# Four expert groups' first products in full float, made during the choice of candidates

## The reference

```python
q = (hx @ w_q)...                                  # 8 heads, two half queries each
s = einsum('thpd,pkd->thpk', q, sub_keys)          # scores against 2 x 128 keys
top_s, top_i = lax.top_k(s, 16)                    # 16 best of each half
cand = top_s[..0.., :, None] + top_s[..1.., None, :]
best_s, best_pos = lax.top_k(cand, 16)             # 16 best of the 256 pairs
wts = softmax(best_s)
act = gelu(einsum('td,thkd->thk', hx, u[idx]))     # first product, rows of u
return einsum('thk,thkd->td', wts * act, v[idx])   # second product, rows of v
```

## Time and profile before

| what | us |
|---|---|
| median of 3 runs | 5012.27 (5011.85 to 5012.48) |
| the profiled execution's own time | 5008.28 |
| its span | 5006.4 |
| TensorE busy in the span | 4576.1 (91%) |
| VectorE busy | 2506.5 (50%) |
| ScalarE busy | 1424.7 (28%) |

### The profile page before, as it was taken

One profiled execution on the slowest core, in us unless ns is written; L12 is line 12 of the kernel. 1 busy time (PEld: TensorE's weight loads), 2 busy tenths in 40 slices (PEclk: granted clock), 3 DMA queues, 4 the chain that ended last, 5 costly groups with the idle time before them and its releaser, 6 DMA issues.

```text
span 5006.4 us, 57535 instructions
## 1 busy us (share of the span) xinstructions
PE 4576.1 (91%) x22736; PEld 3778.7 (75%) x22736; DVE 2506.5 (50%) x4265; ACT 1424.7 (28%) x2544; POOL 0.2 (0%) x4
## 2 busy tenths in 40 slices
PE   6999989999985999998999998909799999999997
PEld 5888877888873458667887887809688888888886
DVE  5666572301013324345776111089566666666665
ACT  1000142200002001234443100117455555555553
POOL 0000000000000000000000000000000000000000
PEclk9999999999997999998999999959899999999999
DMA  7888533245323434120000353302554455554552
GB/s 274 306 305 304 214 130 135 101 135 167 135 101 151 151 116 144 68 87 8 1 1 1 139 164 126 128 7 105 210 199 192 187 212 214 202 200 187 197 214 84
DMA packets 135081, 751.61 MB, mean 150 GB/s; under 512 B 12256, under 2 KB 29792, under 8 KB 66144
## 3 DMA queue, kind: packets, MB, share of 16 engines
q1 hardware_dynamic: 134880, 748.79, 40.6%
HBM read 729.86 MB, written 18.87 MB: 150 GB/s over the span
## 4 chain that ended last, share of the span: by engine, by line
PE 63%; DVE 6%; ACT 2%; issue 1%; DMA 1%; DVEq 0%; SPq 0%; ACTq 0%
PE ps L272 15%; PE ps L2665 14%; PE ps L2641 10%; PE ps L2643 5%; PE ps L759 4%; PE ps L2349 2%; PE ps L2580 1%; PE ps L2179 1%; PE ps L2182 1%; PE ps L2572 1%; PE ps L2170 1%; PE ps L299 1%; PE ps L2228 1%; DVE area L309 1%; PE ps L2227 0%
## 5 line engine op out<-in xcount | busy, mean ns | idle before, releaser
L272 PE MATMUL ps<-area,ring 128*128 128x256 f32 (+1 forms) x5280 | 1283.4, 406 | 50.0 <-ACT area L1413 22.1
L272 PEld LDWEIGHTS ps<-area,ring 128*128 128x128 f32 x5280 | 1006.1, 191 | 327.3 <-issue 201.9
L2641 PE MATMUL ps<-hp_parts,pieces 128*128 128x512 f32 x2048 | 728.7, 400 | 33.3 <-DVE pieces L2737 33.3
L2665 PE MATMUL ps<-pieces,gact_parts 128*128 128x512 f32 x3072 | 706.2, 391 | 5.3 <-issue 2.8
L2665 PEld LDWEIGHTS ps<-pieces,gact_parts 128*128 128x128 f32 x3072 | 576.3, 188 | 127.0 <-DVE pieces L2737 3.7
L676 DVE SCALAR_TENSOR_TENSOR area<-ring,area 128x2048 f32<-128x2048 f32 x192 | 432.4, 2289 | 315.0 <-DMA ring<-w_mod_dram 314.7
L2643 PE MATMUL ps<-hp_parts,pieces 128*128 128x256 f32 x2048 | 576.8, 282 | 0.0
L2737 DVE TENSOR_TENSOR pieces<-ring,pieces 128x512 fp32r<-128x512 f32 x512 | 353.4, 691 | 308.9 <-ACT pieces L2682 308.9
L2641 PEld LDWEIGHTS ps<-hp_parts,pieces 128*128 128x128 f32 x2048 | 386.8, 189 | 129.7 <-issue 25.7
L2682 ACT ACTIVATE pieces<-ring 128x512 fp32r<-128x512 f32 x512 | 323.1, 632 | 400.0 <-PE ps L2643 312.8
L2737 DVE TENSOR_TENSOR pieces<-area,pieces 128x512 fp32r<-128x512 f32 x512 | 352.5, 689 | 162.2 <-ACT pieces L2682 153.5
(11 more groups left out here) (410 smaller groups left out, 4218.0 us busy)
## 6 DMA issues: line engine op xcount, KB each, us to landing
ring<-u_dram SPq DMA_DIRECT2D x128, 1024.0 KB, 7.0
area<-v_dram SPq DMA_DIRECT2D x128, 1024.0 KB, 8.5
ring<-w_mod_dram SPq DMA_DIRECT2D x96, 1024.0 KB, 7.0
ring<-w_mg_dram SPq DMA_DIRECT2D x80, 1024.0 KB, 4.8
ring<-w_z_dram SPq DMA_DIRECT2D x77, 1024.0 KB, 4.9
ring<-w_branch_dram SPq DMA_DIRECT2D x80, 512.0 KB, 3.5
ring<-w_out_dram SPq DMA_DIRECT2D x32, 1024.0 KB, 4.8
ring<-w_y_dram SPq DMA_DIRECT2D x20, 1024.0 KB, 4.8
```

The lines of the kernel that those rows point to most:

```text
L272: last = nc.tensor.matmul(bank(slot, 0, n) if out is None else out, ring[:, slot, k * P:(k + 1) * P], rhs(k), start=(k == 0), stop=(k == k ...
L2641: both = nc.tensor.matmul(bank(s).rearrange("p (a t) -> p a t", t=T), piece[:, b, 0, k * P:(k + 1) * P], hp2[:, :, c, :], start=(c == 0), ...
L2665: last = nc.tensor.matmul(out, gact[:, k, ga, s, t * P:(t + 1) * P], piece[:, b, va, :], start=(s == 0 and w == 0), stop=(s == GROUP - 1 a ...
```

## The change

The u phases of groups 0 to 3 (EARLY = 4) are replaced by float32 products with `hp` itself, which TensorE makes right after the scores. Their sums go to banks 0 to 3 and 4 to 7 in turn; ScalarE takes the GELU of each from PSUM into the buffer `x`, between its Exp instructions. x, the residual, is stored to DRAM before and loaded again in group 4. SyncE loads the u rows of groups 1 to 4 as rows are used up. In the expert stage TensorE's order becomes u4, v0, v1, v2, v3, then u5, v4, u6, v5 and so on to u31, v30, v31. `gact_parts` and `hp_parts` change places in memory, so that of hp_parts only 80 columns of the first quarter still lie in the last weight buffer; the split of hp is made in quarters, in the order 1, 2, 3, 0, and only quarter 0 waits for the last store. The clearing of yacc moves behind the remainders of the first u phase.

```diff
+        EARLY = 4
+        early = x[:, :].rearrange("p (g s t) -> p g s t", g=EARLY, t=T)
-        hp_parts, gact_parts, pieces = ...
+        gact_parts, hp_parts, pieces = ...
 # choose_act
+            def early_gelu(g):
+                act.wait_ge(early_made, GROUP * (g + 1))
+                if g == 0:
+                    act.wait_ge(inputs_loaded, (N_INPUTS + 1) * 16)
+                b = GROUP * (g % 2)
+                nc.scalar.activation(early[:, g, :, :], ps[:, b:b + GROUP, 0:T], ACT.Gelu).then_inc(early_kept, 1)
             for r in range(DC // LANES):
+                for g in {0: (0, 1), 2: (2,)}.get(r, ()):
+                    early_gelu(g)
                 ...
+            early_gelu(3)
 # choose_pe, after the scores
+            for g in range(EARLY):
+                for r in range(GROUP):
+                    pe.wait_ge(u_landed[r], g * 16 + 16)
+                    if r == 0 and g < 2:
+                        S["scores"].upto(pe, "act", f"k{4 * g + 3}", 0)
+                    elif r == 0:
+                        pe.wait_ge(early_kept, g - 1)
+                    for c in range(DC):
+                        last = nc.tensor.matmul(bank(GROUP * (g % 2) + r, 0, T), ring[:, r, c * P:(c + 1) * P], hp[:, c, :], start=(c == 0), stop=(c == DC - 1))
+                    last.then_inc(early_made, 1)
+            pe.wait_ge(early_kept, EARLY)
             barrier(pe, "scores", "cand")
 # experts_act
-            for k in range(2):
-                act.wait_ge(w_stored[k], 32)
-            do("rounded", nc.scalar.activation(hp2[:, 0, :, :], hp, ACT.Copy))
-            u_act(act, 0, 0)
-            keep_half(act, 0, PER_PHASE)
-            gelu_act(act, 0)
+            for q in (1, 2, 3, 0):
+                if q == 0:
+                    act.wait_ge(w_stored[1], 32)
+                do(f"r{q}", nc.scalar.activation(hp2[:, 0, 4 * q:4 * q + 4, :], hp[:, 4 * q:4 * q + 4, :], ACT.Copy))
+            u_act(act, EARLY, 0)
             round_gact(act, 0, 0)
+            keep_half(act, EARLY, PER_PHASE)
+            gelu_act(act, EARLY)
 # experts_dve
-            nc.vector.memset(yacc, 0.0).then_inc(zeroed, 1)
             for n in range(PER_PHASE):
                 remainder(dve, n, n, u_source(n))
-            sum_halves(dve, 0)
+            dve.wait_ge(w_stored[0], 32)
+            nc.vector.memset(yacc, 0.0).then_inc(zeroed, 1)
             weigh(dve, 0, 0)
             split_gact(dve, 0, 0)
+            sum_halves(dve, EARLY)
 # the order of phases: a group has a u phase before its v phase only where
+        def has_u(g):
+            return EARLY <= g < NG - 1
 # experts_sp
             load_u(0)
+            barrier(sp, "norm_p")
+            sp.dma_start(a["residual"], x[:, :]).then_inc(inputs_loaded, 16)
+            for g in range(1, EARLY + 1):
+                load_u(g)               # row s waits for early_made >= 4 * (g - 1) + s + 1
             ...
+                if g == EARLY:
+                    sp.wait_ge(gact_split, EARLY)
+                    sp.dma_start(x[:, :], a["residual"]).then_inc(inputs_loaded, 16)
                 if not is_last(g):
                     sp.wait_ge(remainders, v_base(g) + PER_PHASE)
                     load_v(g + 1)
```

More of the change, by code:

```diff
@@ L2616, in is_last, with u_base, after_early, gelu_of @@
             return g >= NG - n
-        def base(g):
-            return g * (2 * PER_PHASE) + PER_PHASE
+        def has_u(g):
+            return EARLY <= g < NG - 1
+        def u_base(g):
+            return PER_PHASE * (1 + EARLY + 2 * (g - EARLY - 1)) if g > EARLY else 0
         def v_base(g):
-            return base(g) + (0 if is_last(g) else PER_PHASE)
+            if g < EARLY:
+                return PER_PHASE * (1 + g)
+            return PER_PHASE * (1 + EARLY + 2 * (g - EARLY) + has_u(g))
+        def after_early(g):
+            return g - EARLY
+        def gelu_of(g):
+            return early[:, g, :, :] if g < EARLY else gel
         def take_piece(pe, p):
@@ L2725, in group @@
                     round_piece(act, v_base(g) + n, n, v_source(n))
-                    if n == 3 and not is_last(g):
+                    if n == 3 and has_u(g):
                         keep_half(act, g + 1, v_base(g))
-                    if n == 6 and not is_last(g):
+                    if n == 6 and has_u(g):
                         gelu_act(act, g + 1)
@@ L2768, in experts_dve @@
             dve.wait_ge(weights_kept, NR)
-            for k in range(2):
-                dve.wait_ge(w_stored[k], 32)
             do = Do(dve, st_hps, "dve")
-            do.wait("act", "rounded")
-            do("rest", nc.vector.tensor_tensor(hp2[:, 1, :, :], hp, hp2[:, 0, :, :].bitcast(F32), ALU.subtract))
+            for q in (1, 2, 3, 0):
+                do.wait("act", f"r{q}")
+                v = slice(4 * q, 4 * q + 4)
+                do(f"l{q}", nc.vector.tensor_tensor(hp2[:, 1, v, :], hp[:, v, :], hp2[:, 0, v, :].bitcast(F32), ALU.subtract))
             do.end()
-            nc.vector.memset(yacc, 0.0).then_inc(zeroed, 1)
             for n in range(PER_PHASE):
                 remainder(dve, n, n, u_source(n))
-            sum_halves(dve, 0)
+            dve.wait_ge(w_stored[0], 32)
+            nc.vector.memset(yacc, 0.0).then_inc(zeroed, 1)
             weigh(dve, 0, 0)
             split_gact(dve, 0, 0)
+            sum_halves(dve, EARLY)
             dve.wait_ge(zeroed, 1)
             def group(g, k):
-                for n in range(0 if is_last(g) else PER_PHASE):
-                    remainder(dve, base(g) + n, n, u_source(n))
-                    if n == LAG and g > 0:
+                for n in range(PER_PHASE if has_u(g) else 0):
+                    remainder(dve, u_base(g + 1) + n, n, u_source(n))
+                    if n == LAG:
                         add(dve, g - 1, 3)
@@ L2789, in group @@
                     remainder(dve, v_base(g) + n, n, v_source(n))
-                    if is_last(g) and n == LAG:
+                    if not has_u(g) and g > 0 and n == LAG:
                         add(dve, g - 1, 3)
@@ L2793, in group @@
                         add(dve, g, n // GROUP - 1)
-                    if n == 4 and not is_last(g):
+                    if n == 4 and has_u(g):
                         sum_halves(dve, g + 1)
@@ L2804, in last_dve @@
         def last_dve(dve):
+            dve.wait_ge(inputs_loaded, (N_INPUTS + 2) * 16)
             do = Do(dve, st_res, "dve")
@@ L2835, in experts_sp, with load_u @@
             sp.dma_start(cut(PC_AT, N_PEER_CONSTS), a["peer_consts"]).then_inc(peer_loaded, 16)
-            def load_u(g, at=None):
+            def load_u(g):
                 for s in range(GROUP):
-                    if at is not None:
-                        sp.wait_ge(remainders, at + (4 * s + 4))
+                    if g > EARLY:
+                        sp.wait_ge(remainders, u_base(g - 1) + (4 * s + 4))
+                    elif g > 0:
+                        sp.wait_ge(early_made, GROUP * (g - 1) + s + 1)
                     sp.dma_start(ring[:, s, 0:D], a["u"][g * GROUP + s]).then_inc(u_landed[s], 16)
```

43 lines of the change are left out of this document (25 added, 18 removed).

## The result

| | before | after |
|---|---|---|
| timed runs, median | 5012.06 (5006.43 to 5012.48) | 4927.82 (4925.16 to 4930.41) |
| the profiled execution's own time | 5008.28 | 4925.83 |
| its span | 5006.4 | 4924.1 |

The ratio is 0.983, with an interval of 0.982 to 0.985: 84.2 us less by medians, 82.45 by the profiled executions.

The account below looks back on a forecast made before the run. TensorE was taken to bound the queries and expert stage, VectorE the choice. Terms of -90.4, -0.5, -10.1, -1.2, +28.0 and +1.5 gave -72.7 us: 5008.3 becomes 4935.6, plus 4.0 for the median, 4939 (4931 to 4947).

Parts of the forecast that it names:

- A u phase, taken away four times: Expert stage: groups 0 to 3 lose their u phases of 22.59 us each, 90.4 us off.
- The same products in full float: Choice: 110.6 us of float32 products fit into TensorE's idle time, cost 0, with 3.1 us of cover.
- Rival 1: Choice becomes bound a little by ScalarE's order or by TensorE: 10 us on, 4949; chance 0.10.
- Rival 3: Float products in the choice run at the low clock, 221 us: kernel 34 us slower, 5046; chance 0.03.
- Rival 4: Something other than TensorE sets the expert stage: only 10 to 20 us off, about 4997; chance 0.02.
- Rival 2: The v phases wait for whole loads, 13.7 us each instead of 9.85: 11.6 us on, 4951; chance 0.07.
- rival 5: More gain, from v waits nearer to 8 us and a smaller gap: 5 us off, 4934; no separate chance given.
- The split of hp: Before the first expert product: quarters 1 to 3 made under the store, only quarter 0 waits; 10.1 us off.
- What is late next: v: Expert stage: v1, v2, v3 each wait for their load like v31, 28.0 us on, plus 1.5 us.
- The two added halves of a us: Waits of v1 to v3: 0.5 us added each for next group's passes and queued expert weights, 1.5 us on.
- The warm start: Transposes after the choice: TensorE comes to them warm, 0.5 us off.
- The gap behind the first u phase: Expert stage: TensorE's gap shrinks from 7.70 to 6.5 us, 1.2 us off, between 0 and 3.

Follow-up runs that it names:

- the kernel without waits: Changed kernel with v1, v3 and v31 loaded into idle ring slots, and v2, v4 asked for one phase earlier: 4899.21 us, ratio 0.978.
- the kernel before with v31 in the ring: Kernel before, only v31's rows loaded into the ring slots, whose last u rows are used up by then: 4998.98 us, ratio 0.998.

## Why the prediction came out as it did

**Right.** *A u phase, taken away four times:* the expert stage is bound by TensorE, 90.4 booked and 90.7 gone (91.2 in the repeat), both as the remainder; one and two groups show it step by step, within their spread. *The same products in full float:* nothing to pay, with a cover of 3.3 us (3.1 booked) that doubling group 3 measured. The four GELUs start at 3279.59, 3307.22, 3334.85 and 3362.47 where 3280.4, 3308.1, 3335.7 and 3363.4 were forecast. Rival 1 named the mechanism that the earlier GELU then showed, but the order of the change avoids it. Rival 3 falls: the window of the choice has the clock at 1.00. Rival 4 falls with the 90.7. Rival 2 was on the wrong side, and rival 5, waits shorter than v31's, was the right one, with too small a size. *The split of hp:* 10.1 booked, 10.16 measured, 9.6 by medians when alone. VectorE wasn't slowed in the choice by what runs beside it: 106.45 us busy with TensorE busy for 109.59 and DMA at 0.50, and 106.3 without. That is what the Trainium skill's rule on who interferes with whom (SBUF — State Buffer) says, and the trace agrees.

**The step that failed: "What is late next: v".** It booked 3 x 9.35 + 1.5 = 29.5 us; 21.1 were measured, and this is 8.4 of the 9.8 us by which the sum (-72.7, measured -82.45) was off. The mechanism stood: taking the loads' wait away took all of it. The size was read from one phase, v31. Over all kernels with such waits, the one with added matmuls aside, a v phase behind a v phase has one of three lengths:

| length, us | phases | last 78 matmuls | behind how long a last wait | fourth piece begun, after the asking |
|---|---|---|---|---|
| 31.1 to 31.2 | v31 before, after, repeated, with group 3 doubled and with the earlier GELU; v1 of the float products alone and with the earlier GELU | 19.6 | 2.1 to 2.2 | 13.6 to 13.7 |
| 29.4 to 29.7 | v1 after, repeated and with group 3 doubled; v31 of one and two groups, of the split alone and of the float products alone | 18.0 | 1.3 to 2.3 | 13.5 to 13.8 |
| 28.2 to 28.6 | v2 and v3 wherever four groups are early; v1 of two groups | 18.0 | 0.7 to 0.9 | 12.2 to 12.5 |

Two separate things make the steps. The first is 1.6 us of clock *after* the wait. The windows view of the kernel before just behind v31's wait, then that of the float products alone behind v1's:

```profile
4950.00:4957.00 7.00, 6.94 (x23) 5.56 (x24) 4.63 (x9) 2.73 (x5) 0.00 (x0) 0.76 0.00 0
```

```profile
3591.00:3598.00 7.00, 6.94 (x23) 5.57 (x24) 5.33 (x9) 2.74 (x5) 0.00 (x0) 0.76 0.00 0
```

Both have 0.76 there, and 19.6 us for 78 matmuls; the changed kernel's v1 has 1.00 and 17.98. The second is the fourth row of v. SyncE asks for v1's rows and v2's rows at

```profile
3567.86 1.95 SPq L2895 DMA_DIRECT2D area<-v_dram  x4
3597.49 1.97 SPq L2895 DMA_DIRECT2D area<-v_dram  x4
```

and ScalarE begins the first and the fourth piece of each phase at

```profile
3572.86 0.63 ACT L2718 ACTIVATE pieces<-area 128x512 fp32r<-128x512 f32 x1 [6.29 <-DMA area<-v_dram]
3581.59 2.20 ACT L2718 ACTIVATE pieces<-area 128x512 fp32r<-128x512 f32 x4 [3.11 <-DMA area<-v_dram]
3602.33 0.63 ACT L2718 ACTIVATE pieces<-area 128x512 fp32r<-128x512 f32 x1 [6.12 <-DMA area<-v_dram]
3609.86 2.20 ACT L2718 ACTIVATE pieces<-area 128x512 fp32r<-128x512 f32 x4 [1.90 <-DMA area<-v_dram]
```

The first piece comes 5.00 and 4.84 us after the asking, but the fourth 13.73 and 12.37. This step is worth 1.2 to 1.4 us of the phase. The two together leave nothing over: in all 29 such phases of the traces, those with added matmuls included, the length is the time from the asking to the fourth piece plus 15.9 to 16.3 us, or plus 17.5 where the clock fell. So v31's 9.35 is 6.5 plus 1.2 plus 1.6; v2 and v3 have neither surcharge, v1 one.

The trace of before held both already. In its v31 ScalarE begins the third and the fourth piece at

```profile
4944.92 0.63 ACT L2682 ACTIVATE pieces<-area 128x512 fp32r<-128x512 f32 x1 [1.86 <-DMA area<-v_dram]
4948.65 2.19 ACT L2682 ACTIVATE pieces<-area 128x512 fp32r<-128x512 f32 x4 [3.10 <-DMA area<-v_dram]
```

which is 3.73 us apart where the pieces ahead are 2.5 apart, and 19.60 us for 78 matmuls stand against 17.7, their share of 21.79. Without these two the wait would have been an estimated 6.2 us instead of 9.35. The range's lower bound, 3 x 8 = 24, took off less than that and gave no reason. The two added halves of a us (the next group's split, the expert weights in the queue) don't show: v2, which has both, waits for 6.5 us in all. Why the fourth row lands later in some phases, and why the clock falls behind the same wait of 2.08 us in one kernel and not in another, isn't settled by these runs.

**Smaller misses.** *The warm start:* 0.5 booked, 1.65 measured between the transposes and the last store, but 0.09 in the same kernel repeated, 0.04 with the float products alone. In 3380:3384 the granted clock is 0.90 after; the same window of the kernel before has 0.50:

```profile
3380.00:3384.00 4.00, 4.00 (x21) 4.00 (x20) 4.00 (x7) 1.19 (x2) 0.00 (x0) 0.50 0.00 0
```

The gain lies in rounds that run at the higher clock. As it came in one execution of this kernel and not in another, it is not shown to belong to the change. *The gap behind the first u phase:* 1.2 booked, 0.53 measured (7.76, then 7.23). The u phase ahead of it took 0.40 us longer than before and 0.37 less in the repeat, so only 0.13 came off by this stretch of the first trace. That this shortfall and the surplus of the warm start nearly cancel in the sum is luck. The clearing is in this gap now, with a pause of 0.80 ahead of it that the prediction had weighed elsewhere. VectorE's row:

```profile
3536.82 3.47 DVE L2817 MEMSET area<- 128x4096 f32 x1 [0.80 <-issue]
```

The kernel with the float products alone shows that the clearing's move itself costs 2.4 us, which the split pays for. *The distance of the median from the profiled execution:* 4.0 was added. The kernel before has times in two clusters some 5.5 us apart (5006.1 to 5008.3 and 5011.4 to 5013.7); the three runs shown were of the upper, the profile of the lower. The median after lies 2.0 above its profile, which accounts for the remaining 2 us of the miss. The other 0.8 us arose ahead of the choice, where nothing was changed.

## What to carry to other kernels

A wait read from a single phase has a size with a history. Take it apart before it is multiplied: how far apart do its rows land, and at what clock does the work behind it run? What looks unlike its neighbours (here a row 3.7 us behind the last where others are 2.5, and 19.6 us for matmuls that are worth 17.7) may be missing at the next place, so the wait without it is one end of the range. When phases of one stream are pulled out of an alternation, the other stream's buffers become the bound; look for slots that the first stream no longer uses before the waits are accepted (26 us here). A product that costs more on its engine is free in another engine's stage as long as the cover is counted to its end and the instructions between the two engines keep their order: 3.3 us of cover, and 4.7 us lost by one GELU a round too early.

## What the runs showed of the hardware

- The two clusters of times seem to part before the choice. The first u row is asked for at 3242.5 to 3244.8 in eleven of the thirteen traces, and at 3249.12 in the kernel without waits and 3248.91 in the kernel before with v31 in the ring, whose code ahead of it is the same as in others. Both of these profiles are among the longer times of their kernel. Nothing of a change in the expert stage explains it, and a comparison of spans has to take it out.
- The same 78 matmuls behind the same idle time of 2.08 us took 19.60 us in v31 of the kernel before, at a granted clock of 0.76 in the first 7 us, and 17.97 in v31 with one early group.
- Four 1 MB rows asked for together land some 4.9, 7.4, 9.9 and 12.4 or 13.6 us later, by the start of ScalarE's first pass over each. The rate in the wait of v1 is 422 GB/s, again as the earlier trace rows, with one core at work, above the 358 of the Trainium skill (SBUF — State Buffer, "A bandwidth-pool intuition that's wrong"); the measurement decides.
- A load of ScalarE's table costs its 1.28 us and no more: in the kernel with the earlier GELU the load starts 0.03 us behind the end of the GELU, at 3335.90, and the Exp starts at 3337.19, 1.29 us behind the start of the load. The Trainium skill (ScalarE: Activation LUTs, "What ACT_TABLE_LOAD costs") adds a drain of 1.38 us, which this trace doesn't show.
